# Eight expert weight slots in place of six, with the loop's buffers in the mixer's feature buffer

## The chip, the cores and the metric

The kernel runs on one core of a Trainium2 chip. The metric is device time in microseconds of one launch; three runs of the kernel before gave 1341.48, 1341.05 and 1335.37 us, median 1341.05. One execution more was taken with the hardware profiler; every row below comes from it.

## The reference

Two layers of a hybrid trunk over 384 tokens (128 context, 256 latent) with 1024 features. Each layer has a token mixer (layer 0: a gated linear recurrence beside a long convolution; layer 1: two kinds of attention) and then a mixture of experts, which is what the change touches. All values are fp32.

```python
def hier_moe(h, w_grp, b_grp, w_rt, b_rt, w_gate, w_up, w_down):
    t = h.reshape(B * L, D)
    g_p, g_i = lax.top_k(jax.nn.softmax(t @ w_grp + b_grp), 1)      # 1 of 4 groups
    e_p, e_i = lax.top_k(softmax(logits of that group), TOP_K)      # 2 of its 4 experts
    ...
    a = jnp.einsum('td,edf->tef', t, w_gate)
    u = jnp.einsum('td,edf->tef', t, w_up)
    hid = jax.nn.silu(a) * u * gates[..., None]
    y = jnp.einsum('tef,efd->td', hid, w_down)
```

There are 16 experts a layer, each with three weight matrices of 1024 x 512 (gate, up) and 512 x 1024 (down).

## The kernel before

*Weight blocks.* All weights come in blocks of 128 x 4096 fp32 (2.097 MB), moved by SP's DMA queue. The mixers' projections and the adaLN weights (`in_proj`, 41 blocks) go through `ring`, three slots in turn (`load_blocks`, L531 to 543). An expert is three blocks (gate, up, down) of `in_moe`; a layer has 48 of them. Even experts use the three slots of `ring`, odd experts three more, `mo["ring"]`, which lie in `arena`, a scratch area of 22616 columns that the mixers use before (`carve`, L327). So six blocks can be held.

*Order of the loads* (`load_experts`, L545 to 580). The first block into `ring` waits for the last reader of one of its slots; then SP waits until the mixer's features are done (`features_mixed`) and an output has left the arena, issues three loads into the arena, and then two more into `ring` as its slots come free. After `table_ready` (the table of the first chunk of each expert) a loop over seven pairs of experts reloads a slot as soon as the expert that used it has passed the matmuls of that block (`gate_full`, `up_full`, `down_full`). SP is one queue in program order: a load behind a wait goes no earlier than that wait ends.

*Rows.* Tokens are routed to experts in chunks of 64 rows (`CAP`). POOL scatters all rows to `slots` in DRAM by an indirect DMA (L622), then loads chunk by chunk 64 x 1024 into `mo["rows"]` (L626, L634, L631), stores the results back (L639), and at the end gathers each token's two results (L648) into `picked`, on top of the arena slots. An expert has one or more chunks, by the data; a layer has 19 here.

*One chunk on the engines.* PE: 16 matmuls with the gate block and 16 with the up block (L1602; an fp32 matmul shows as two passes, so 64 rows), `turn` of the next chunk's rows by transposes (L1578), transposes of the hidden values (L1608), 8 matmuls with the down block (L1617, 16 passes). ScalarE copies the turned rows to `hS` (L785), applies SiLU (L794), copies the transposed hidden values (L800) and the output (L806). VectorE multiplies (L1291) and has nothing else in the loop. POOL may reload `rows` only when PE has turned both halves (`turned`, L630), and PE asks for the next chunk's rows ahead of the last step of the up block:

```python
if kind == 1 and k == KD - 1:
    pe.wait_ge(sems["rows_in"], g * 16 + 32)
```

PE and SP run a loop over pairs of experts around loops over chunks (L1588, L574); the loop bounds are read from the table (`first_chunk`, L516). After the loop PE transposes the token sums back (L1626) and VectorE adds them to `xT` (L1302). `cT` is the mixer's feature buffer, 3072 columns: the output projection (L1797) reads it last, and after the loop VectorE builds the token sums in it (L1296, L1297).

After layer 0's loop, SP loads layer 1's first three projection blocks (L540) as the last readers of `ring`, those of expert 14, are done.

Of the kernel before, what the change touches and what calls it, by code (L numbers as in the profile page):

```python
# [28 lines left out]
F32 = mybir.dt.float32  # L29
# [39 lines left out]
PROJ_SLOTS = 3  # L69

# [227 lines left out]
def trunk_kernel(nc, params_d, hypar_d, consts_d, hyconst_d, x_d, s0_d, ck_d, cv_d, dk_d, dv_d,  # L298
                 proj_d, moe_d, y_d, state_d, ock_d, ocv_d, odk_d, odv_d, slots_d):
    banks = plan_banks()  # L300
    with ExitStack() as ctx:
# [25 lines left out]
        def carve(shapes):  # L327

            out, at = {}, 0
            for name, shape in shapes:  # L330
# [4 lines left out]
                elif len(shape) == 3:  # L335
# [25 lines left out]
        mo = carve([("ring", (3, KD * HALF)), ("hS", (KD, CAP)), ("sg", (FHALF,)), ("hid", (FHALF,)),  # L361
                    ("hidT", (2, P)), ("rows", (D,)), ("out", (HALF,)), ("rk", (T,)),
# [5 lines left out]
                    ("posi", (TOP_K * NT,)), ("prime", (2,))])  # L368
        picked = mo["ring"].rearrange("p r n -> p (r n)")[:, 0 : TOP_K * NT * D].rearrange("p (s d) -> p s d", d=D)
# [6 lines left out]
        slot_loaded = [sem(f"slot_loaded{s}") for s in range(2 * PROJ_SLOTS)]  # L376
# [20 lines left out]
        loop_names = ("rows_in", "turned", "hS_ready", "gate_full", "up_full", "sg_ready", "hid_ready", "hidT_full",  # L397
# [86 lines left out]
        def slot_of(n):  # L484
# [3 lines left out]
            earlier = sum(1 for m in range(first) if m % PROJ_SLOTS == s) + (NE // 2 if layer else 0)  # L488
# [14 lines left out]
        def moe_block(side, kind):  # L503

            return (mo["ring"] if side else ring)[:, kind, :]

        def moe_loaded(side, kind):
            return slot_loaded[PROJ_SLOTS * side + kind]

        def moe_loads(layer, side, kind):  # L510

            if side:
                return layer * NE // 2
            return sum(slot_of(n)[0] == kind for n in range(sum(LAYER_BLOCKS[: layer + 1]))) + layer * NE // 2
# [9 lines left out]
        def _(sp):  # L524
# [1488 lines left out]
```

## Time and profile before

| what | value |
|---|---|
| three runs, median | 1341.05 us |
| the profiled execution, its own time | 1336.44 us |
| its span, first to last instruction | 1334.8 us |
| PE busy, matmuls | 1087.7 us |
| ScalarE, VectorE, POOL busy | 381.7, 319.8, 118.3 us |
| mean granted TensorE clock | 0.937 |
| DMA | 341.58 MB, 256 GB/s over the span |

Outside its span the profiled execution has 1.64 us. The page gives busy times for the whole span; its 40 slices of 33 us show two long stretches in which the DMA digit is 9, the two expert loops (L1602 starts at 469.57 us in layer 0 and at 1039.91 us in layer 1). Busy PE is not PE at its peak, and a share of the whole is a mean over stages. In the chain of waits each step names what the next one waited for; in the timelines a bracket behind a row gives the engine's idle time ahead of it and what ended it.

### The profile page before, as it was taken

To read this page: it belongs to the slowest core of one execution; us is meant where nothing else is said; L and a number is where in the kernel's file an instruction comes from. 1 tells how busy PE (TensorE), PEld (TensorE's weight loads), DVE (VectorE), ACT (ScalarE), POOL (GpSimd) and SP (SyncE) were. 2 spreads that over 40 slices of the span, in tenths; PEclk is the share of its full clock that TensorE was granted. 3 is DMA by queue.
4 is the path that set the end of the run, shared out by engine and by line. 5 is a ranking of instruction groups with operands and counts; after the bars stand their busy time and mean duration, and the time that the engine had idled before them with its cause. 6 is when DMAs were issued, how large, how long until landed. Compare 5 with 4: busy or idle time off the path is not lost.

```text
span 1334.8 us, 16405 instructions
## 1 busy us (share of the span) xinstructions
PE 1087.7 (81%) x6064; PEld 617.9 (46%) x6065; DVE 319.8 (24%) x869; ACT 381.7 (29%) x729; POOL 118.3 (9%) x201
## 2 busy tenths in 40 slices
PE   4899999889898299777997279899893897799991
PEld 1444545446454155444664044455551454365651
DVE  3332132433443200000000054555524000000003
ACT  4221101432323122122232046554632222222220
POOL 0000002000100211000110210000001010011112
PEclk9999999999999789888999689999996899999995
DMA  9644417641925749999999802221072699999984
GB/s 368 285 189 189 189 63 305 270 189 64 379 88 228 314 155 398 394 401 399 387 386 397 314 25 109 88 80 63 1 309 114 262 389 397 406 391 385 383 335 149
DMA packets 35287, 341.58 MB, mean 256 GB/s; under 512 B 4912, under 2 KB 6064, under 8 KB 17328
## 3 DMA queue, kind: packets, MB, share of 16 engines
q1 hardware_dynamic: 21744, 295.97, 56.0%
q0 software_dynamic: 13504, 45.10, 9.4%
q8 instruction: 24, 0.39, 0.1%
q14 instruction: 15, 0.12, 0.0%
HBM read 313.00 MB, written 28.05 MB: 256 GB/s over the span
## 4 chain that ended last, share of the span: by engine, by line
PE 57%; DMA 24%; DVE 7%; ACT 5%; issue 4%; POOL 2%; POOLq 0%; DVEq 0%; SPq 0%; ACTq 0%
PE bank L1602 12%; PE bank L1531 10%; DMA arena<-in_moe 10%; PE bank L1523 8%; DMA ring<-in_moe 6%; PE bank L1797 6%; PE bank L1617 5%; DMA arena<-slots 3%; DMA ring<-in_proj 2%; PE bank L1494 2%; PE bank L1508 2%; PE bank L1719 2%; DMA arena<-slots,arena 1%; POOL slots L622 1%; PE bank L1500 1%
## 5 line engine op out<-in xcount | busy, mean ns | idle before, releaser
L1531 PE MATMUL bank<-ring,hT 128*128 128x512 f32 x384 | 169.8, 597 | 5.5 <-ACT hT L732 4.3
L1602 PE MATMUL bank<-arena 128*64 128x256 f32 x1216 | 143.4, 392 | 27.2 <-DMA arena<-in_moe 25.4
L1602 PE MATMUL bank<-ring,arena 128*64 128x256 f32 x1216 | 146.1, 398 | 23.6 <-DMA ring<-in_moe 20.2
L1291 DVE TENSOR_TENSOR arena<-bank,arena 128x256 f32<-128x256 f32 x38 | 16.1, 425 | 545.2 <-PE bank L1602 545.2
L1602 PEld LDWEIGHTS bank<-arena 128*64 128x64 f32 x1216 | 100.5, 141 | 75.3 <-DMA arena<-in_moe 23.4
L1602 PEld LDWEIGHTS bank<-ring,arena 128*64 128x64 f32 x1216 | 101.3, 144 | 72.1 <-DMA ring<-in_moe 22.3
L1531 PEld LDWEIGHTS bank<-ring,hT 128*128 128x128 f32 x384 | 72.3, 192 | 91.7 <-issue 88.6
L1523 PE MATMUL bank<-hT,ring 128*128 128x384 f32 x320 | 108.0, 498 | 4.5 <-ACT hT L732 2.5
L785 ACT ACTIVATE arena<-bank 128x256 f32<-128x256 f32 x80 | 30.6, 383 | 234.3 <-PE bank L1578 234.0
L1797 PE MATMUL bank<-cT,ring 128*128 128x384 f32 x256 | 84.6, 487 | 0.0
L1523 PEld LDWEIGHTS bank<-hT,ring 128*128 128x128 f32 x320 | 61.9, 195 | 48.7 <-issue 6.5
L1617 PE MATMUL bank<-ring,arena 128*64 128x512 f32 x304 | 71.1, 609 | 3.0 <-DMA ring<-in_moe 0.9
L1617 PE MATMUL bank<-arena 128*64 128x512 f32 x304 | 69.4, 597 | 2.5 <-DMA arena<-in_moe 0.2
L1578 PE MATMUL bank<-con,arena 64*128 64x64 f32 x320 | 37.2, 239 | 41.5 <-DMA arena<-slots 41.5
L1797 PEld LDWEIGHTS bank<-cT,ring 128*128 128x128 f32 x256 | 47.9, 190 | 32.1 <-issue 0.9
L806 ACT ACTIVATE arena<-bank 128x512 f32<-128x512 f32 x38 | 22.7, 597 | 134.6 <-PE bank L1617 134.6
L1578 PEld LDWEIGHTS bank<-con,arena 64*128 64x128 f32 x320 | 26.5, 142 | 62.6 <-issue 62.6
L1626 PE MATMUL bank<-con,cT 128*128 128x128 f32 x48 | 9.7, 395 | 54.9 <-DVE cT L1297 54.9
L639 POOL DMA_DIRECT2D slots<-arena x76 | 40.8, 537 | 152.0 <-ACT arena L806 149.9
L794 ACT ACT_TABLE_LOAD x38 | 48.8, 1283 | 1.5 <-issue 0.8
L631 POOL DMA_DIRECT2D arena<-slots x38 | 20.0, 527 | 326.1 <-PE bank L1578 318.0
L1494 PE MATMUL bank<-ring,condT 128*32 128x512 f32 x384 | 46.3, 598 | 0.0
(268 smaller groups left out, 1134.9 us busy)
## 6 DMA issues: line engine op xcount, KB each, us to landing
ring<-in_moe SPq DMA_DIRECT2D x48, 2048.0 KB, 21.0
arena<-in_moe SPq DMA_DIRECT2D x48, 2048.0 KB, 22.4
ring<-in_proj SPq DMA_DIRECT2D x41, 2048.0 KB, 10.2
arena<-slots POOLq DMA_DIRECT2D x42, 256.0 KB, 8.8
slots<-arena POOLq DMA_DIRECT2D x76, 128.0 KB, 7.4
slots<-blank POOLq DMA_DIRECT2D x1, 7680.0 KB, 38.3
arena<-in_hyconst SPq DMA_DIRECT2D x1, 2432.0 KB, 14.7
xT<-in_x SPq DMA_DIRECT2D x1, 1536.0 KB, 11.5
```

What stands on the lines that cost most here:

```text
L639: pool.dma_start(slots_d[bass.ds(g * CAP, CAP), HALF * half : HALF * half + HALF], mo["out"][CAP * half : CAP * half + CAP, :]).then_inc(s ...
L785: nc.scalar.activation(mo["hS"][:, 4 * half : 4 * half + 4, :], psum[ROWS_BANK + half][:, 0 : 4 * CAP].rearrange("p (k n) -> p k n", k=4), ...
L794: nc.scalar.activation(mo["sg"], psum[GATE_BANK][:, 0:FHALF], ACT.Silu).then_inc(sems["sg_ready"], 1)
L1494: ins = mm(ps[rows, :], condT[:, k, :], w[:, k, :], start=k < 4, stop=k >= 4)
L1508: ins = mm(ps[:, 0:T], ones, hT[:, k, :], start=k == 0, stop=k == KD - 1)
L1523: ins = mm(ps[:, 0:T], w[:, k, P * m : P * m + P], src[:, k, :], start=k == 0, stop=k == KD - 1)
L1531: ins = mm(ps[:, :], src[:, k, P * i : P * i + P], w[:, k, :], start=k == 0, stop=k == KD - 1)
L1578: ins = nc.tensor.transpose(psum[ROWS_BANK + half][:, CAP * k : CAP * k + CAP], mo["rows"][0:CAP, P * (4 * half + k) : P * (4 * half + k) ...
L1602: ins = mm(psum[kind][CAP * half : CAP * half + CAP, 0:FHALF], mo["hS"][:, k, :], wk[:, k, FHALF * half : FHALF * half + FHALF], start=k = ...
L1617: ins = mm(psum[DOWN_BANK][CAP * half : CAP * half + CAP, :], mo["hidT"][:, b, CAP * fh : CAP * fh + CAP], wd[:, 2 * fh + b, HALF * half : ...
L1719: mm(ps[:, :], sc["el"][:, b, h, :], sc["vx"][:, h].rearrange("p j n -> p (j n)"), start=True, stop=True).then_inc(full_of("scan", u, f"U{ ...
L1797: ins = mm(ps[:, 0:T], w[:, k, P * j : P * j + P], cT[:, 4 * half + k, :], start=k == 0, stop=k == 3)
```

## The change

- `mo["ring"]` grows from three to five slots, so that with `ring` eight blocks are held (`MOE_SLOTS`). Block n of a layer's 48 goes to slot n modulo 8: five arena slots first, then the three of `ring` in the order in which its last projection blocks end (`ring_order`).
- `rows`, `hS`, `sg`, `hid` and `rk` move from the arena into `cT`. A new buffer `land` lies there too.
- Row loads go to `land`; VectorE copies `land` to `rows` once PE has turned the chunk before (`copy_rows`); POOL loads the next chunk when the copy is done, and PE waits for the copy.
- The loops over pairs are written out: PE has 16 loops over chunks, one for each expert, SP has 40 loads with fixed addresses.
- The first eight loads: SP waits for the mixer's features and the output's store first, issues the five arena loads, then the three into `ring`, each when its slot's last reader is done.
- Layer 1's first projection blocks now wait for expert 15, whose blocks lie in `ring`.
- `slots` has two chunks more, and they are cleared with the others; one row load more is issued a layer.

```diff
+ARENA_SLOTS = 5
+MOE_SLOTS = ARENA_SLOTS + PROJ_SLOTS
+MOE_BLOCKS = 3 * NE
...
-        mo = carve([("ring", (3, KD * HALF)), ("hS", (KD, CAP)), ("sg", (FHALF,)), ("hid", (FHALF,)),
-                    ("hidT", (2, P)), ("rows", (D,)), ("out", (HALF,)), ("rk", (T,)),
+        mo = carve([("ring", (ARENA_SLOTS, KD * HALF)), ("hidT", (2, P)), ("out", (HALF,)),
                     ("lg", (NT, 20)), ("l8", (NT, 8)), ("m8", (NT, 8)), ("i8", (NT, 8)), ("f8", (NT, 8)),
...
+        features = cT[:, :, :].rearrange("p k t -> p (k t)")
+        mo["rows"], mo["land"] = features[:, 0:D], features[:, D : 2 * D]
+        mo["hS"] = features[:, 2 * D : 2 * D + KD * CAP].rearrange("p (k n) -> p k n", k=KD)
+        mo["sg"] = features[:, 2 * D + KD * CAP : 2 * D + KD * CAP + FHALF]
+        mo["hid"] = features[:, 2 * D + KD * CAP + FHALF : 3 * D]
+        mo["rk"] = features[:, 2 * D + KD * CAP : 2 * D + KD * CAP + T]
         picked = mo["ring"].rearrange("p r n -> p (r n)")[:, 0 : TOP_K * NT * D].rearrange("p (s d) -> p s d", d=D)
...
+        def ring_order(layer):
+            end = sum(LAYER_BLOCKS[: layer + 1])
+            return [slot_of(n)[0] for n in range(end - PROJ_SLOTS, end)]
+        def moe_slot(layer, n):
+            v = n % MOE_SLOTS
+            return PROJ_SLOTS + v if v < ARENA_SLOTS else ring_order(layer)[v - ARENA_SLOTS]
+        def moe_block(layer, n):
+            v = n % MOE_SLOTS
+            return mo["ring"][:, v, :] if v < ARENA_SLOTS else ring[:, moe_slot(layer, n), :]
+        def moe_loads(layer, n):
+            s = moe_slot(layer, n)
+            proj = sum(slot_of(m)[0] == s for m in range(sum(LAYER_BLOCKS[: layer + 1])))
+            return proj + (layer * MOE_BLOCKS + n) // MOE_SLOTS + 1
...
-                def load(pair, kind, side):
-                    at_block = pair * 6 + (layer * NE * 3 + 3 * side + kind)
-                    sp.dma_start(moe_block(side, kind),
-                                 moe_d[bass.ds(at_block, 1)].rearrange("o p n -> p (o n)")).then_inc(moe_loaded(side, kind), 16)
-                def load_first(kind):
-                    full(sp, *last_group(last[kind]))
-                    load(0, kind, 0)
-                order = sorted(range(3), key=lambda kind: STREAM.index(last[kind]))
-                load_first(order[0])
+                sems = loops[layer]
+                def load(n):
+                    sp.dma_start(moe_block(layer, n),
+                                 moe_d[layer * MOE_BLOCKS + n]).then_inc(slot_loaded[moe_slot(layer, n)], 16)
                 features_mixed(sp, layer)
                 if layer == 0:
                     sp.wait_ge(state_out, 32)
                 else:
                     sp.wait_ge(cache_out, 64)
-                for kind in range(3):
-                    load(0, kind, 1)
-                for kind in sorted(order[1:]) if layer == 0 else order[1:]:
-                    load_first(kind)
-                sems = loops[layer]
+                for n in range(MOE_SLOTS):
+                    if n >= ARENA_SLOTS:
+                        full(sp, *last_group(last[moe_slot(layer, n)]))
+                    load(n)
                 sp.wait_ge(table_ready, layer + 1)
-                with sp.Fori(1, NPAIR) as i:
-                    for side in range(2):
-                        done = first_chunk(sp, i * 2 + (side - 1))
-                        for kind in range(3):
-                            sp.wait_ge(sems[("gate_full", "up_full", "down_full")[kind]], done)
-                            load(i, kind, side)
-                return first_chunk(sp, NE - 1)
+                ends = {}
+                for n in range(MOE_SLOTS, MOE_BLOCKS):
+                    expert, kind = (n - MOE_SLOTS) // 3, (n - MOE_SLOTS) % 3
+                    if kind == 0:
+                        ends[expert] = first_chunk(sp, expert + 1)
+                    sp.wait_ge(sems[("gate_full", "up_full", "down_full")[kind]], ends[expert])
+                    load(n)
+                return first_chunk(sp, NE)
...
+            def experts_done(slot):
+                kind = ring_order(0).index(slot)
...
-                pool.dma_start(mo["rows"][0:CAP, :], slots_d[0:CAP, :]).then_inc(sems["rows_in"], 16)
+                def load_rows(chunk):
+                    pool.dma_start(mo["land"][0:CAP, :], slots_d[bass.ds(chunk * CAP, CAP), :]).then_inc(sems["rows_in"], 16)
+                load_rows(0)
                 chunks = first_chunk(pool, NE)
-                def load_rows(chunk):
-                    pool.wait_ge(sems["turned"], chunk * 2)
-                    pool.dma_start(mo["rows"][0:CAP, :], slots_d[bass.ds(chunk * CAP, CAP), :]).then_inc(sems["rows_in"], 16)
-                pool.wait_ge(sems["turned"], 2)
-                pool.dma_start(mo["rows"][0:CAP, :], slots_d[CAP : 2 * CAP, :]).then_inc(sems["rows_in"], 16)
+                for chunk in (1, 2):
+                    pool.wait_ge(sems["rows_copied"], chunk)
+                    load_rows(chunk)
                 with pool.Fori(0, chunks) as g:
-                    load_rows(g + 2)
+                    pool.wait_ge(sems["rows_copied"], g + 3)
+                    load_rows(g + 3)
...
+                def copy_rows(chunk):
+                    dve.wait_ge(sems["rows_in"], chunk * 16 + 16)
+                    V.tensor_copy(mo["rows"][0:CAP, :], mo["land"][0:CAP, :]).then_inc(sems["rows_copied"], 1)
+                copy_rows(0)
+                dve.wait_ge(sems["turned"], 2)
+                copy_rows(1)
                 with dve.Fori(0, first_chunk(dve, NE)) as g:
                     dve.wait_ge(sems["hidT_full"], g + 1)
                     dve.wait_ge(sems["sg_ready"], g + 1)
                     dve.wait_ge(sems["up_full"], g + 1)
                     V.tensor_tensor(mo["hid"], psum[UP_BANK][:, 0:FHALF], mo["sg"], ALU.mult).then_inc(sems["hid_ready"], 1)
+                    dve.wait_ge(sems["turned"], g * 2 + 4)
+                    copy_rows(g + 2)
...
-                def weights_loaded(pair, kind, side):
-                    pe.wait_ge(moe_loaded(side, kind), pair * 16 + 16 * (moe_loads(layer, side, kind) + 1))
-                pe.wait_ge(sems["rows_in"], 16)
...
+                pe.wait_ge(sems["rows_copied"], 1)
...
+                for e in range(NE):
+                    w = [moe_block(layer, 3 * e + kind) for kind in range(3)]
+                    with pe.Fori(first_chunk(pe, e), first_chunk(pe, e + 1)) as g:
+                        for kind, done in ((0, "gate_full"), (1, "up_full")):
+                            weights_loaded(3 * e + kind)
...
+                                    pe.wait_ge(sems["rows_copied"], g + 2)
```

How instructions stand now, at three places. SP ahead of layer 0's loop (`bank_free` and `state_out` stand for the mixer's features and the output's store, each `bank_full` for the last matmuls of a block that held the slot); before:

```order
L540 DMA ring<-in_proj 128x4096 [waits bank_full5]
L551 DMA ring<-in_moe 128x4096 [waits bank_full5]
L551 DMA arena<-in_moe 128x4096 [waits bank_free0,state_out,bank_free4,bank_free3]
L551 DMA arena<-in_moe 128x4096 x2
L551 DMA ring<-in_moe 128x4096 [waits bank_full1]
L551 DMA ring<-in_moe 128x4096 [waits bank_full7]
L574 UNCONDITIONAL_BRANCH [waits table_ready]
```

and now:

```order
L556 DMA ring<-in_proj 128x4096 [waits bank_full5]
L567 DMA arena<-in_moe 128x4096 [waits bank_free0,state_out,bank_free4,bank_free3]
L567 DMA arena<-in_moe 128x4096 x4
L567 DMA ring<-in_moe 128x4096 [waits bank_full5]
L567 DMA ring<-in_moe 128x4096 [waits bank_full7]
L567 DMA ring<-in_moe 128x4096 [waits bank_full1]
L534 TENSOR_LOAD arena [waits table_ready]
```

The arena's loads have moved ahead of the first `ring` slot's wait, and are five. VectorE in layer 1's loop (`up_full`, `sg_ready`, `hidT_full` are the matmuls, the SiLU and the bank of the hidden values); before:

```order
L1286 UNCONDITIONAL_BRANCH
L1286 ISA
L1291 TENSOR_TENSOR arena<-bank,arena 128x256 [waits up_full1,sg_ready1,hidT_full1]
L1286 REGISTER_ALU
L1286 COMPARE_AND_BRANCH
```

and now, from the copies ahead of the loop on:

```order
L1300 COPY cT<-cT 64x1024 [waits rows_in1,dve_link]
L1300 COPY cT<-cT 64x1024 [waits rows_in1,turned1]
L534 TENSOR_LOAD arena
L534 ISA x2
L1305 UNCONDITIONAL_BRANCH
L1305 ISA
L1310 TENSOR_TENSOR cT<-bank,cT 128x256 [waits up_full1,sg_ready1,hidT_full1]
L1311 ISA
L1299 ISA [waits turned1]
L1300 COPY cT<-cT 64x1024 [waits rows_in1]
L1305 REGISTER_ALU
L1305 COMPARE_AND_BRANCH
```

A copy with two waits has come behind each multiplication, and the next multiplication stands behind it. POOL in layer 0 from the first row load on; before:

```order
L626 DMA arena<-slots 64x1024 [waits rows_placed]
L518 TENSOR_LOAD arena
L518 ISA x2
L634 DMA arena<-slots 64x1024 [waits turned0]
L635 UNCONDITIONAL_BRANCH
L635 ISA
L631 ISA [waits turned0]
L631 DMA arena<-slots 64x1024
L639 ISA [waits out_ready0]
L639 DMA slots<-arena 64x512
```

and now:

```order
L637 DMA cT<-slots 64x1024 [waits rows_placed]
L534 TENSOR_LOAD arena
L534 ISA x2
L637 DMA cT<-slots 64x1024 [waits rows_copied0] x2
L644 UNCONDITIONAL_BRANCH
L644 ISA
L637 ISA [waits rows_copied0]
L637 DMA cT<-slots 64x1024
L647 REGISTER_ALU
L649 ISA [waits out_ready0]
L649 DMA slots<-arena 64x512
```

Each row load waits for VectorE's copy in place of PE's turn, and one load more goes ahead of the loop.

## Rows read from the trace of the kernel before

**Rows 1.** The page, parts 1 and 4: PE's busy time; chain by engine.

```profile
PE 1087.7 (81%) x6064; PEld 617.9 (46%) x6065; DVE 319.8 (24%) x869; ACT 381.7 (29%) x729; POOL 118.3 (9%) x201
...
PE 57%; DMA 24%; DVE 7%; ACT 5%; issue 4%; POOL 2%; POOLq 0%; DVEq 0%; SPq 0%; ACTq 0%
```

**Rows 2.** Windows: stretch, length, busy of PE, PEld, DVE, ACT, POOL; clock, DMA, GB/s.

```profile
500.00:740.00 240.00, 207.14 (x1494) 122.27 (x1492) 7.22 (x17) 56.15 (x100) 26.24 (x49) 0.96 1.01 395
1060.00:1290.00 230.00, 203.16 (x1506) 123.72 (x1504) 7.22 (x17) 57.64 (x101) 27.10 (x51) 0.99 1.01 394
```

**Rows 3.** The chain that ended last, layer 0's loop: start us, us, what.

```profile
668.33 3.65 PE bank L1617 x16
...
680.47 3.65 PE bank L1617 x16
...
703.36 28.93 DMA arena<-in_moe
...
737.60 3.67 PE bank L1617 x16
...
743.21 8.73 DMA slots<-arena
```

**Rows 4.** The same chain, the end of layer 1's loop.

```profile
1298.05 3.68 PE bank L1617 x16
1303.67 2.47 DMA slots<-arena
```

**Rows 5.** Waits of PE in layer 0's loop: us in total, times, longest us.

```profile
PE bank L1602 <- DMA arena<-in_moe: 14.3, 5, 3.3
PE bank L1602 <- DMA ring<-in_moe: 11.7, 4, 3.0
PE bank L1608 <- DVE arena L1291: 4.4, 19, 0.2
```

**Rows 6.** Waits of PE in layer 1's loop.

```profile
PE bank L1602 <- DMA arena<-in_moe: 11.0, 5, 3.2
PE bank L1602 <- DMA ring<-in_moe: 8.5, 4, 2.9
...
PE bank L1602 <- DMA arena<-slots: 2.6, 3, 1.2
```

**Rows 7.** Timeline of SP's queue at five places: start us, us from first to last.

```profile
418.11 0.33 SPq L551 DMA_DIRECT2D ring<-in_moe  x1
418.62 1.36 SPq L551 DMA_DIRECT2D arena<-in_moe  x3
442.64 0.80 SPq L551 DMA_DIRECT2D ring<-in_moe  x2
...
488.03 0.34 SPq L551 DMA_DIRECT2D ring<-in_moe  x1
...
711.88 12.37 SPq L540 DMA_DIRECT2D ring<-in_proj  x3
...
1046.09 3.77 SPq L551 DMA_DIRECT2D ring<-in_moe  x2
```

**Rows 8.** Timeline of POOL, scatter and first row load, layer 0 and layer 1.

```profile
448.90 1.04 POOL L622 DMA_INDIRECT slots<-hT,arena  x1 [30.46 <-DVE arena L1263]
...
463.70 0.58 POOL L626 DMA_DIRECT2D arena<-slots  x1 [6.87 <-DMA slots<-hT,arena]
...
1023.30 1.00 POOL L622 DMA_INDIRECT slots<-hT,arena  x1 [27.74 <-DVE arena L1263]
...
1034.46 0.55 POOL L626 DMA_DIRECT2D arena<-slots  x1 [3.26 <-DMA slots<-hT,arena]
```

**Rows 9.** Timeline of VectorE behind layer 0's gather.

```profile
765.48 0.75 DVE L1296 TENSOR_SCALAR cT<-arena 128x1024 f32<-128x1024 f32 x1 [28.89 <-DMA arena<-slots,arena]
```

**Rows 10.** The page, part 3, DMA queues: packets, MB, share of 16 engines.

```profile
q8 instruction: 24, 0.39, 0.1%
```

**Rows 11.** Timeline of PE, the first matmuls of layer 0's expert 1.

```profile
496.33 6.67 PE L1602 MATMUL bank<-arena 128*64 128x256 f32 x60
```

More of the change, by code:

```diff
@@ L375, in trunk_kernel @@
         s0_in, caches_in = sem("s0_in"), sem("caches_in")
-        slot_loaded = [sem(f"slot_loaded{s}") for s in range(2 * PROJ_SLOTS)]
+        slot_loaded = [sem(f"slot_loaded{s}") for s in range(MOE_SLOTS)]
         bank_full = [sem(f"bank_full{b}") for b in range(BANKS)]
@@ L487, in slot_of @@
             s = (n - first) % PROJ_SLOTS
-            earlier = sum(1 for m in range(first) if m % PROJ_SLOTS == s) + (NE // 2 if layer else 0)
+            earlier = sum(1 for m in range(first) if m % PROJ_SLOTS == s) + (MOE_BLOCKS // MOE_SLOTS if layer else 0)
             return s, earlier + (n - first) // PROJ_SLOTS + 1
@@ L501, in last_group @@
             return (*name, KD - 1)
[L503 to L514, printed above, removed]
+        def ring_order(layer):
[11 more added lines that the diff above has]
+            return proj + (layer * MOE_BLOCKS + n) // MOE_SLOTS + 1
         def first_chunk(eng, expert):
@@ L1580, in turn, with weights_loaded @@
                     ins.then_inc(sems["turned"], 1)
[L1582 to L1585 removed]
+                def weights_loaded(n):
+                    pe.wait_ge(slot_loaded[moe_slot(layer, n)], 16 * moe_loads(layer, n))
+                pe.wait_ge(sems["rows_copied"], 1)
                 for half in range(2):
                     turn(half)
[L1588 to L1619 removed]
@@ new lines, in experts @@
+                for e in range(NE):
[3 more added lines that the diff above has]
+                            weights_loaded(3 * e + kind)
+                            wk = w[kind].rearrange("p (k n) -> p k n", k=KD)
+                            for k in range(KD):
+                                if kind == 0 and k % 4 == 0:
+                                    pe.wait_ge(sems["hS_ready"], g * 2 + (k // 4 + 1))
+                                if kind == 1 and k == KD - 1:
+                                    pe.wait_ge(sems["rows_copied"], g + 2)
+                                for half in range(2):
+                                    ins = mm(psum[kind][CAP * half : CAP * half + CAP, 0:FHALF], mo["hS"][:, k, :],
+                                             wk[:, k, FHALF * half : FHALF * half + FHALF], start=k == 0, stop=k == KD - 1)
+                            ins.then_inc(sems[done], 1)
+                        turn(0)
+                        pe.wait_ge(sems["hid_ready"], g + 1)
+                        for b in range(2):
+                            ins = nc.tensor.transpose(psum[HIDT_BANK][:, P * b : P * b + P], mo["hid"][:, P * b : P * b + P], ident)
+                        ins.then_inc(sems["hidT_full"], 1)
+                        turn(1)
+                        weights_loaded(3 * e + 2)
+                        pe.wait_ge(sems["hidT_ready"], g + 1)
+                        pe.wait_ge(sems["out_ready"], g + 1)
+                        wd = w[2].rearrange("p (f n) -> p f n", f=NF)
+                        for n, (b, fh) in enumerate(((0, 0), (0, 1), (1, 0), (1, 1))):
+                            for half in range(2):
+                                ins = mm(psum[DOWN_BANK][CAP * half : CAP * half + CAP, :], mo["hidT"][:, b, CAP * fh : CAP * fh + CAP],
+                                         wd[:, 2 * fh + b, HALF * half : HALF * half + HALF], start=n == 0, stop=n == NF - 1)
+                        ins.then_inc(sems["down_full"], 1)
@@ L2005 @@
     args += [nc.dram_tensor("out_" + n, s, F32, kind="ExternalOutput").ap() for n, s in outs.items()]
-    slots = nc.dram_tensor("slots", (CAP * (MAX_CHUNKS + 2), D), F32, kind="Internal").ap()
+    slots = nc.dram_tensor("slots", (CAP * (MAX_CHUNKS + 4), D), F32, kind="Internal").ap()
     trunk_kernel(nc, *args, slots)
```

37 lines of the change are left out of this document (3 added, 34 removed).

## Prediction

> **What bounds the kernel now.** The page comes first: TensorE is busy 81% of the span, and the chain that ended last is 57% PE and 24% DMA [rows 1]. Such a share is a mean over stages, so the two expert loops, where nearly all the edits lie, are read by themselves. The reader should look at the last two columns of the windows: over 240 us of layer 0's loop and 230 us of layer 1's, the DMA engines are busy all the time (1.01) and move 395 and 394 GB/s, while PE has 207 of 240 and 203 of 230 us [rows 2]. So the transfers fill the loop, and PE doesn't. The waits of PE say the same from the other side: it stands 14.3 + 11.7 = 26.0 us for weight blocks in layer 0's loop and 11.0 + 8.5 = 19.5 us in layer 1's [rows 5, 6]. The chain shows it where it counts, at the end: in layer 0 a weight transfer of 28.93 us stands ahead of the last chunk, whose last matmuls start at 737.60; in layer 1 they start at 1298.05 [rows 3, 4].
>
> A balance of bytes tests this reading. The first refill of a slot is issued at 488.03 in layer 0 and at 1046.09 in layer 1 [rows 7]; all loads issued earlier had landed while PE was still on its first chunks. After it 48 - 6 = 42 blocks of 128 x 4096 fp32 (2.097 MB) must come, 2.097 / 0.395 = 5.31 us each, 223.0 us. The 19 chunks of a layer (PE waits 19 times for the hidden values [rows 5]) each read and write 64 rows of 4 KB, 0.524 MB or 1.33 us, 25.2 us. Together 248.2 us. Measured from first refill to last down projection: 737.60 - 488.03 = 249.6 us and 1298.05 - 1046.09 = 252.0 us. The loop lasts as long as its bytes.
>
> **The change, part by part.**
>
> *Eight slots.* Eight blocks are now loaded ahead of the loop, so 40 and not 42 come after the first refill: 2 x 5.31 = 10.6 us less in each layer, **-21.2 us**. Two things must hold. First, the two extra blocks must fit where the DMA is idle. In layer 0 the five arena loads no longer stand behind a ring slot's last reader, the output projection that let the first loads go at 418.11 and 418.62 [rows 7]; at the earliest they can follow the last projection block. The last two ring slots are still freed at 442.64 at the latest, and what comes after them is two blocks, about 11 us, against the first refill at 488.03. In layer 1 the eighth block has from the output projection to 1046. Second, PE must not become the bound. A chunk takes 680.47 - 668.33 = 12.14 us where nothing is late [rows 3], and of the 26.0 and 19.5 us of waits 15.4 and 8.9 are left after 10.6 are gone. That is cover enough.
>
> *Less crowding ahead of layer 0's loop.* The scatter of rows starts at 448.90 and the first row load goes at 463.70, 14.8 us later; in layer 1 it takes 1034.46 - 1023.30 = 11.2 us [rows 8]. The difference of 3.6 us is the weight blocks: those issued at 442.64 still run during layer 0's scatter. Now the arena's five have gone earlier and only about half a block is left. Ends: 0 and -3.6; I take **-3.0**, near the second, since layer 1's row is the same scatter with a free DMA.
>
> *Rows landed, then copied.* The first chunk's rows now pass VectorE before PE turns them: one copy of 64 x 1024 fp32 a layer on the path. The nearest row is VectorE's 128 x 1024 fp32 operation with one input, 0.75 us [rows 9]; with a hop, 0.85. Ends: half of it, as for half the partitions, and double. Two layers: **+1.7** (0.8 to 3.4). The other copies lie in VectorE's loop behind the turn. They have most of a chunk before PE asks for the rows, and VectorE has 7.22 us of work in 240 [rows 2]. POOL's load of the next rows waits for the copy, about 0.85 us later than for the turn, and the store behind it on POOL waits longer for ScalarE's output anyway: nothing. A row load may now take a whole chunk. It ended PE's waits for 2.6 us in layer 1 [rows 6]; that goes, but the next wait, for weights, comes last: nothing, at most -3.
>
> *Layer 1's first projection blocks.* Before, SP issued three of them from 711.88 on [rows 7], behind the last expert's blocks. Now the last expert sits in the ring, and all three wait for its down projection, since the first in SP's order does. They then cross the last store, which took 8.73 us in layer 0 beside such blocks but 2.47 in layer 1 without [rows 3, 4], and the gather behind it. The store already paid; the gather now pays too, for at most the part of 3 x 5.31 = 15.9 us that outlasts the store, shared half: 0 to +4, I take **+1.0**, since most of it passes during the store. The projection itself comes after gather, token sums and norm, with its weights there.
>
> *Experts written out, the blank rows, buffers moved.* PE loses the backward branch of the pair loop and SP its address arithmetic, neither on a path that ends anything. Clearing 0.5 MB more of rows is 1.3 us of transfer, hidden in the scans. The loop buffers sit in the mixer's features, which are dead between the output projection and the token sums. All 0, with +1 as the end for the clearing. New code must be fetched, though: see the second rival.
>
> Sum: -21.2 - 3.0 + 1.7 + 1.0 = **-21.5 us**. Against the profiled execution's 1336.44 that is 1314.9. The runs shown have their median 4.6 us above it (1341.05, from 1335.37 to 1341.48); not knowing on which side the next median falls I add half, 2.3 us: **1317 us**, and 2.3 is added to the rivals as well.
>
> One rule bears on the size of the main term. The loops move 395 and 394 GB/s [rows 2], and 5.31 us a block comes from that. The Trainium skill ("DMA: Bandwidth & Descriptors", Specifications) states a limit of about 358 GB/s from memory for one core; by it the two blocks would be an estimated 11.7 us a layer and the sum -23.7. The rows are above that limit, so they decide.
>
> **Rivals.**
>
> *PE partly takes over.* The waits left, 15.4 and 8.9 us, hold only if chunks stay at 12.14 us. If fresh code costs PE 1 us an expert, 16 us a layer, the layers gain 26.0 - 16 = 10 and 19.5 - 16 = 3.5 us; with the small terms -13.8, 1325 us. For it: layer 1's margin is thin. Against: nothing yet shows such a stall.
>
> *Instruction fetch ends up slower.* Before, two expert bodies were run eight times; now PE runs sixteen in a row, each for the first time, while the DMA is full. If PE stood at each for a small transfer's trip, for which the nearest row is the 2.47 us of the last store [rows 4], a layer would pay 16 x 2.47 = 39.5 us. It turns slower where that passes the waits it can hide in: above 26.0/16 = 1.6 us an expert in layer 0 and 19.5/16 = 1.2 in layer 1. At 2.47 it is +13.5 and +20.0, with the small terms +33, 1372 us. For it: 24 instruction fetches in the whole run now, and many more then [rows 10]. Against: the second body was fresh once, at 496.33 with the DMA full, and its matmuls show no idle time ahead of them [rows 11]. The Trainium skill ("Runtime: NRT & Kernel Launch", Instruction fetch mechanics) says that prefetch is sequential and that a taken branch out of the window stalls; by that rule written-out code is the safe form, and the row agrees.
>
> *More than the bytes.* Row waits, and PE's slower matmuls behind a weight wait, also go from the end of the chain: about 5 us more, 1312 us.
>
> *The slots don't help.* If the DMA fell idle in the loop because a slot is freed late, or the two blocks were not loaded ahead, the loop would start with the same debt: 1338 us. Against: the issue order gives the arena five loads without a wait among them.
>
> **How the numbers follow.** Forecast 0.65, more than the bytes 0.08, PE partly takes over 0.14, no help 0.07, slower 0.06. A measurement of this kernel can tell about 0.5%, 6.7 us, from no change. The forecast, the larger gain and nearly all of the partial one lie beyond: faster 0.86; same 0.08; slower 0.06. The range takes in the forecast with its ends (all low terms: -21.2 - 3.6 + 0.8 - 3 = -27; all high: -21.2 + 3.4 + 4 + 1 = -12.8), on either level of the runs shown, and the partial case: 1308 to 1328.
>
> **What would show it.** Right: eight weight loads issued before the first refill and 40 after, DMA share 1.0 at about 395 GB/s until the end, first refill to last down projection about 239 us, PE's waits for weights down by about 10 us a layer, the first row load 11 to 12 us after the scatter begins. Wrong: idle gaps of PE at each expert's first matmul that no transfer ends, a DMA share below 1 in the loop, row loads or copies ending PE's waits, or a tail of layer 0 longer by over 4 us.

## The result and the profile after

The kernel after takes 1327.78 us (median of seven runs, 1323.98 to 1330.71), the kernel before 1340.80 (seven runs); ratio 0.9916, 95% interval 0.9897 to 0.9935. It is faster, by 0.84% or 11.3 us, where 21.5 were forecast. (The two medians lie 13.0 us apart; from here on the text goes by the ratio.) The profiled execution of after has a span of 1325.9 us.

The page of after, busy time and the DMA queue that fetches instructions [rows 1, 10]:

```profile
PE 1085.3 (82%) x6064; PEld 618.7 (47%) x6064; DVE 348.5 (26%) x911; ACT 381.8 (29%) x729; POOL 119.2 (9%) x203
...
PE 59%; DMA 24%; DVE 7%; ACT 5%; issue 3%; POOL 2%; POOLq 0%; DVEq 0%; ACTq 0%
...
q8 instruction: 46, 0.75, 0.2%
```

SP's queue around layer 0's loop and at the start of layer 1's, as [rows 7]:

```profile
399.58 2.44 SPq L567 DMA_DIRECT2D arena<-in_moe  x5
419.72 25.70 SPq L567 DMA_DIRECT2D ring<-in_moe  x3
487.69 12.46 SPq L567 DMA_DIRECT2D arena<-in_moe  x4
...
734.02 1.28 SPq L556 DMA_DIRECT2D ring<-in_proj  x3
...
1042.53 15.92 SPq L567 DMA_DIRECT2D arena<-in_moe  x5
```

Eight loads go ahead of the first refill, as said; five of them 19 us earlier than the first arena load of before. The chain that ended last, layer 0's end and layer 1's [rows 3, 4]:

```profile
687.34 36.36 DMA ring<-in_moe
723.74 5.03 PE bank L1622 x32
...
730.33 3.67 PE bank L1637 x16
...
735.95 7.75 DMA slots<-arena
...
751.04 8.60 DMA arena<-slots,arena
```

```profile
1282.44 5.38 PE bank L1622 x32
...
1289.39 3.67 PE bank L1637 x16
...
1295.01 2.45 DMA slots<-arena
```

So a weight transfer still stands ahead of layer 0's last chunk. From first refill to last down projection it is now 730.33 - 487.69 = 242.6 us and 1289.39 - 1042.53 = 246.9; before 249.6 and 252.0, forecast about 239. The loops got 6.9 and 5.1 us shorter, not 10.6 each. The windows of exactly these stretches, with the columns of [rows 2]:

```profile
487.69:730.33 242.64, 212.07 (x1572) 128.69 (x1569) 19.30 (x35) 59.27 (x106) 27.31 (x51) 0.98 0.99 384
1042.53:1289.39 246.86, 220.15 (x1663) 135.30 (x1659) 20.40 (x37) 62.69 (x112) 28.76 (x54) 0.99 0.99 379
```

The same stretches of before:

```profile
488.03:737.60 249.57, 216.36 (x1572) 128.70 (x1568) 7.65 (x18) 59.12 (x106) 27.30 (x51) 0.96 1.01 393
1046.09:1298.05 251.96, 222.63 (x1661) 135.91 (x1656) 8.07 (x19) 62.59 (x112) 28.75 (x54) 0.99 1.00 387
```

The last column is what to read: fewer bytes had to come, but they came at 384 and 379 GB/s in place of 393 and 387, with the DMA engines nearly as busy (0.99 against 1.01 and 1.00). Part of that lies at the loop's ends: from 500 to 720 us it is 392 against 394, from 1060 to 1280 us 387 against 393. PE's waits for weights tell the same; layer 0, then layer 1 [rows 5, 6]:

```profile
PE bank L1622 <- DMA arena<-in_moe: 16.3, 7, 3.6
PE bank L1622 <- DMA ring<-in_moe: 7.7, 3, 3.2
```

```profile
PE bank L1622 <- DMA arena<-in_moe: 9.6, 4, 3.5
PE bank L1622 <- DMA ring<-in_moe: 9.2, 4, 3.4
```

24.0 and 18.8 us, from 26.0 and 19.5: they have hardly fallen, where the prediction wanted about 10 less a layer. The waits for rows (0.5 and 2.6 us) are gone; most of what else the loops lost is PE's own time, 212.07 against 216.36 us and 220.15 against 222.63 for the same matmuls, in layer 0 at a higher granted clock (0.98 against 0.96). POOL's scatter and first row load [rows 8]:

```profile
452.31 1.04 POOL L632 DMA_INDIRECT slots<-hT,arena  x1 [32.27 <-DVE arena L1273]
...
463.48 0.56 POOL L637 DMA_DIRECT2D cT<-slots  x1 [3.24 <-DMA slots<-hT,arena]
```

11.2 us in place of 14.8. (What lies ahead of the scatter differs from one profiled execution to the next: over all kernels of this text it began between 446 and 454 us. So stretches are compared, not times from the start.)

### The profile page after: what moved, and what is told of

Read it like the earlier page. It is cut to its first block, busy times and chain, and to the rows that moved or that the text cites. A ratio compares the mean times of both kernels' runs of the same rounds, so it can differ in the third digit from the quotient of the medians.

```text
span 1325.9 us, 16236 instructions
## 1 busy us (share of the span) xinstructions
PE 1085.3 (82%) x6064; PEld 618.7 (47%) x6064; DVE 348.5 (26%) x911; ACT 381.8 (29%) x729; POOL 119.2 (9%) x203
## 4 chain that ended last, share of the span: by engine, by line
PE 59%; DMA 24%; DVE 7%; ACT 5%; issue 3%; POOL 2%; POOLq 0%; DVEq 0%; ACTq 0%
PE bank L1622 12%; DMA arena<-in_moe 11%; PE bank L1552 11%; PE bank L1544 8%; DMA ring<-in_moe 7%; PE bank L1637 6%; PE bank L1817 6%; DMA ring<-in_proj 2%; PE bank L1515 2%; PE bank L1529 2%; PE bank L1739 2%; DMA arena<-slots,arena 1%; POOL slots L632 1%; PE bank L1521 1%; PE bank L1674 1%
## 5 line engine op out<-in xcount | busy, mean ns | idle before, releaser
L1622 PE MATMUL bank<-arena,cT 128*64 128x256 f32 x1632 | 190.3, 390 | 27.4 <-DMA arena<-in_moe 25.9
L1622 PEld LDWEIGHTS bank<-arena,cT 128*64 128x64 f32 x1632 | 135.2, 141 | 87.8 <-issue 26.2
L1622 PE MATMUL bank<-ring,cT 128*64 128x256 f32 x800 | 93.7, 389 | 16.9 <-DMA ring<-in_moe 16.9
L795 ACT ACTIVATE cT<-bank 128x256 f32<-128x256 f32 x80 | 30.7, 384 | 218.1 <-PE bank L1599 217.8
L1622 PEld LDWEIGHTS bank<-ring,cT 128*64 128x64 f32 x800 | 65.8, 140 | 47.4 <-DMA ring<-in_moe 14.8
L1599 PE MATMUL bank<-con,cT 64*128 64x64 f32 x320 | 37.2, 239 | 39.6 <-DVE cT L1300 39.6
L1637 PE MATMUL bank<-ring,arena 128*64 128x512 f32 x240 | 54.8, 597 | 2.7 <-DMA ring<-in_moe 0.9
L637 POOL DMA_DIRECT2D cT<-slots x44 | 23.2, 527 | 356.7 <-DVE cT L1300 350.2
L1599 PEld LDWEIGHTS bank<-con,cT 64*128 64x128 f32 x320 | 26.5, 142 | 60.8 <-issue 60.8
L1300 DVE COPY cT<-cT 64x1024 f32<-64x1024 f32 x42 | 28.8, 685 | 75.9 <-PE bank L1599 38.1
## 6 DMA issues: line engine op xcount, KB each, us to landing
xT<-in_x SPq DMA_DIRECT2D x1, 1536.0 KB, 11.2
```

The lines of the kernel that those rows point to most:

```text
L795: nc.scalar.activation(mo["hS"][:, 4 * half : 4 * half + 4, :], psum[ROWS_BANK + half][:, 0 : 4 * CAP].rearrange("p (k n) -> p k n", k=4), ...
L1300: V.tensor_copy(mo["rows"][0:CAP, :], mo["land"][0:CAP, :]).then_inc(sems["rows_copied"], 1)
L1599: ins = nc.tensor.transpose(psum[ROWS_BANK + half][:, CAP * k : CAP * k + CAP], mo["rows"][0:CAP, P * (4 * half + k) : P * (4 * half + k) ...
L1622: ins = mm(psum[kind][CAP * half : CAP * half + CAP, 0:FHALF], mo["hS"][:, k, :], wk[:, k, FHALF * half : FHALF * half + FHALF], start=k = ...
L1637: ins = mm(psum[DOWN_BANK][CAP * half : CAP * half + CAP, :], mo["hidT"][:, b, CAP * fh : CAP * fh + CAP], wd[:, 2 * fh + b, HALF * half : ...
```

## The experiments

Each ratio is a kernel's time over that of the kernel before, run in the same round on the same chip. The rounds did not all run on one chip, so kernels of different rounds are compared by their ratios.

**First round: the change taken apart.** Theory: what the two extra slots give is about as forecast, and some other part of the change costs what is missing. Four kernels.

*six_slots*: the changed kernel with the old number of slots.

```diff
-ARENA_SLOTS = 5
+ARENA_SLOTS = 3
```

> The changed kernel with six slots in place of eight; all its other edits stay. From first refill to last down projection the kernel before took 249.6 us (layer 0) and 252.0 us (layer 1), the changed kernel 242.6 and 246.9, where 239 and 241 were forecast. Theory 'the other edits slow the transfers' (instruction fetch or row copies): the two loops come out 3 to 5 us longer than in the kernel before, 253 to 257 us, and the kernel is 0 to 1% slower than before. Rival 'eight blocks outstanding slow the transfers': the loops are as in the kernel before, 250 and 252 us, at 392 to 395 GB/s, and the time is within 0.3% of before.

1346.14 us, ratio 1.0044 (1.0022 to 1.0066): slower than before. Its loops are 252.2 and 258.0 us long, so with eight slots they are 9.5 and 11.1 us shorter: the main term of the sum (10.6 each) was right, and the rest of the change, forecast at -0.3 us, costs 0.44%.

*written_out_alone*: the kernel before, with PE's and SP's loops over pairs written out.

```diff
-                with sp.Fori(1, NPAIR) as i:
+                for i in range(1, NPAIR):
...
-                with pe.Fori(0, NPAIR) as i:
+                for i in range(NPAIR):
```

> The kernel before with its experts written out on TensorE and SP, six slots, nothing else. Theory 'instruction fetch takes from the transfers': about 22 fetches of 16 KB more, loops of 253 to 257 us in place of 249.6 and 252.0, GB/s in the loops down from 393 to 388, the kernel 6 to 9 us slower than before. Rival 'depth' and rival 'row copies': the same as before within 2 us, loops 250 and 252 us.

1344.74 us, 1.0037 (1.0016 to 1.0059). The edit that was priced at 0 costs about 5 us.

*landed_alone*: the kernel before, with `land`, VectorE's copies and the row loads that wait for them (the buffers stay in the arena).

```diff
+                    dve.wait_ge(sems["turned"], g * 2 + 4)
+                    copy_rows(g + 2)
...
-                    load_rows(g + 2)
+                    pool.wait_ge(sems["rows_copied"], g + 3)
+                    load_rows(g + 3)
```

> The kernel before with rows landed and then copied by VectorE, nothing else. If the copies or the earlier row loads disturb the weight transfers: loops of 253 to 257 us, the kernel 6 to 9 us slower. If they don't: the two first copies alone, 1 to 2 us slower than before, loops 250 and 252 us.

1340.35 us, 0.9998 (0.9972 to 1.0024): the copies cost nothing that can be told (the interval is -3.8 to +3.2 us, so the 1.7 us forecast fit as well).

*late_projection*: the changed kernel; SP holds layer 1's first projection loads until the gather has landed.

```diff
                 kind = ring_order(0).index(slot)
+                sp.wait_ge(picked_in, 16 * TOP_K * NT)
```

> The changed kernel, with layer 1's first three projection blocks loaded only after layer 0's gather has landed. In the changed kernel the last store took 7.75 us and the last gather 8.60 us behind its issue; in layer 1, with no such blocks, 2.45 and 6.52. Theory 'these blocks stand in the way of the tail': store 2.5 and gather 6.5, layer 0's tail 7 us shorter, the kernel 6 to 8 us faster than the changed one. Rival: the projection then waits for its weights (a block lands about 7 us after its issue) and takes the gain back; no more than 2 us faster.

1314.21 us, 0.9803 (0.9774 to 0.9832): ahead of both kernels, and of after by 1.1% in the ratio. SP and POOL behind layer 0's loop in it:

```profile
753.67 1.28 SPq L556 DMA_DIRECT2D ring<-in_proj  x3
```

```profile
740.11 0.19 POOL L654 TENSOR_TENSOR arena<-arena 128x1 f32<-128x1 f32 x1 [2.17 <-DMA slots<-arena]
```

and POOL at the same place in after:

```profile
743.95 0.19 POOL L653 TENSOR_TENSOR arena<-arena 128x1 f32<-128x1 f32 x1 [7.46 <-DMA slots<-arena]
```

In after the three blocks are issued at 734.02, ahead of the last store (735.95), so the store takes 7.75 us and the gather is crossed too. With them held, the wait for the store falls from 7.46 to 2.17 us and the stretch from the gather's first issue to the token sums from 15.0 (744.68 to 759.66) to 12.8. That is 7.4 us of the chain; layer 1's projection begins no later for it. The ratio shows more than these 7.4 us (1.1%, some 15). The profiled execution was the longest of its six, 1320.98 us, 6.5 below that of after. The granted clock goes along with the rest: the four shortest runs of late_projection (1311.63 to 1314.45) have a mean of 0.940 to 0.943, the two longest 0.933 and 0.934, after's seven 0.926 to 0.939. Whether the clock is the cause is open.

**Second round: which part of writing out.** Theories: instruction fetches, which come with PE's sixteen bodies; or SP's loads; or the buffers' place, since six_slots has a longer layer 1 loop than written_out_alone.

*pe_written_out* (only the PE line of the diff of written_out_alone):

> The kernel before with only PE's loop over pairs written out; SP keeps its loop. Question: writing out PE and SP together cost 0.37% (about 5 us) where the prediction had 0. Theory A (instruction fetch): the whole price comes with PE, since PE's sixteen bodies are the code that is new: 1343 to 1346 us, instruction fetches up from 24 to about 46, PE idle no longer at an expert's first matmul, the loops 2 to 3 us longer in total. Rival B (SP's written-out loads are the price, for instance because they are issued in another rhythm): 1340 to 1341 us, loops as before.

1345.49 us, 1.0038 (1.0015 to 1.0061), 46 fetches in place of 24.

*sp_written_out* (only the SP line):

> The kernel before with only SP's loop over pairs written out (fixed addresses); PE keeps its loop. Theory A (instruction fetch by PE's bodies): no change, 1339 to 1342 us, and at most a few more instruction fetches. Rival B (SP's loads are the price): 1343 to 1346 us.

1339.11 us, 1.0003 (0.9977 to 1.0029), 24 fetches. By these two the price is PE's.

*buffers_moved_alone*:

```diff
-        mo = carve([("ring", (3, KD * HALF)), ("hS", (KD, CAP)), ("sg", (FHALF,)), ("hid", (FHALF,)),
-                    ("hidT", (2, P)), ("rows", (D,)), ("out", (HALF,)), ("rk", (T,)),
+        mo = carve([("ring", (3, KD * HALF)), ("hidT", (2, P)), ("out", (HALF,)),
+        features = cT[:, :, :].rearrange("p k t -> p (k t)")
+        mo["rows"] = features[:, 0:D]
...
```

> The kernel before with rows, hS, sg, hid and rk in the mixer's feature buffer and nothing else changed. The change with six slots has 386 GB/s in layer 1's loop and a loop 6 us longer than before, the written-out kernel alone 392 and 0.8 us. Theory A (the buffers' place costs nothing, as predicted): 1339 to 1342 us, 393 to 395 GB/s in both windows. Rival C (the buffers' new place slows layer 1): 1344 to 1346 us, about 387 GB/s in layer 1's window.

1341.01 us, 1.0012 (0.9989 to 1.0035): nothing that can be told.

*late_projection_eight_bodies*: late_projection, with PE's experts as a loop of two over eight bodies (block n + 24 has the slot of block n, so eight is the smallest number with eight slots).

```diff
-                for e in range(NE):
+                with pe.Fori(0, 2) as i:
+                    for e in range(NE // 2):
```

> The changed kernel with layer 1's first three projection loads held until the gather has landed (1314.21 us by itself), and PE's sixteen experts as a loop of two over eight bodies, so that half of the code is new in each layer. Theory A (instruction fetch): fetches fall from 46 to about 34 and the loops get 1 to 3 us shorter in total, 1311 to 1313 us, a version ahead of both kernels. Rival D (the price isn't the code that is fetched): 1314 to 1315 us, or longer if the backward branch costs.

1316.81 us, 0.9812 (0.9772 to 0.9852), 34 fetches: no gain over late_projection. With 0.4% to either side the run could not have told the 1 to 3 us that were expected, so it decides nothing.

**Third round: PE's bodies in the changed kernel, and what a transfer on one engine costs.**

*six_slots_pair_loop*: six_slots with PE's loop over pairs put back, everything else as changed.

```diff
-                for e in range(NE):
+                with pe.Fori(0, NPAIR) as i:
+                    for e in range(2):
```

> The changed kernel with six slots (1346.14 us, ratio 1.0044) and PE's experts as the loop over eight pairs that the kernel before has; the moved buffers, landed rows, load order and SP's written-out loads stay. Theory A (PE's sixteen bodies are the price that the prediction set to 0): the 5 us go, and with the less crowded scatter that this kernel keeps it comes to 1338 to 1341 us, instruction fetches back to 24, each loop 250 to 252 us. Rival E (the price lies in the moved buffers, the copies and the load order taken together, since layer 1's loop took 258 us with six slots and 254 at most with PE written out alone): 1344 to 1346 us, layer 1's loop still 256 us or longer.

1336.93 us, 0.9981 (0.9966 to 0.9997): 9.2 us below six_slots, 8.4 by the ratios. Sixteen bodies are what the change loses by. The loops took 249.7 and 254.1 us in it, 252.2 and 258.0 in six_slots, though PE was busy for 6.4 us less in those; pe_written_out has 253.1 and 254.5, sp_written_out 250.5 and 251.5. (Layer 1's 254.1 is above the 250 to 252 expected.) PE's waits in layer 1 (1050 to 1285 us), in six_slots:

```profile
PE bank L1622 <- DMA arena<-in_moe: 12.9, 5, 3.8
PE bank L1622 <- DMA ring<-in_moe: 5.9, 3, 3.2
PE bank L1628 <- DVE cT L1310: 3.9, 17, 0.2
PE bank L1637 <- DMA arena<-in_moe: 2.0, 2, 1.9
PE bank L1637 <- DMA ring<-in_moe: 1.3, 2, 1.1
```

and in six_slots_pair_loop:

```profile
PE bank L1623 <- DMA arena<-in_moe: 9.8, 4, 3.1
PE bank L1623 <- DMA ring<-in_moe: 6.2, 2, 3.2
PE bank L1629 <- DVE cT L1310: 3.9, 17, 0.2
```

22.1 us of waits for weights against 16.0. PE does not stand at a new body; it stands for weights that come later. (The waits alone would be a weak sign: they also grow when PE runs at a higher clock, and sp_written_out, which costs nothing, has 20.9 us of them in this stretch at a clock of 1.00.) The windows, 500 to 720 and 1060 to 1280 us, six_slots:

```profile
500.00:720.00 220.00, 184.63 (x1350) 108.43 (x1348) 16.65 (x30) 51.20 (x90) 24.10 (x45) 0.97 1.01 393
1060.00:1280.00 220.00, 192.70 (x1418) 115.59 (x1416) 17.75 (x32) 53.11 (x95) 24.94 (x48) 0.97 1.01 386
```

and six_slots_pair_loop:

```profile
500.00:720.00 220.00, 192.90 (x1384) 113.94 (x1382) 16.64 (x30) 53.13 (x92) 25.74 (x48) 0.95 1.01 397
1060.00:1280.00 220.00, 198.06 (x1441) 121.57 (x1442) 17.90 (x33) 54.99 (x97) 25.58 (x48) 0.96 1.01 391
```

397 and 391 GB/s against 393 and 386, at the same DMA share. These two kernels ran on different chips; on one chip, pe_written_out has 391 and 393 in the two windows and sp_written_out 392 and 393, so the lower rate is not shown to be the code's. Nor do the loops hold all of the price: of the 9.9 us between the two spans 6.4 lie in the loops and 3.5 ahead of the scatter, where no expert body has run yet; pe_written_out and sp_written_out differ by 5.6 us in the loops and 7.1 ahead of the scatter. Whether the part ahead is a difference between executions or belongs to the code is open. In the trace eleven more fetches lie in each loop, packets of 16.4 KB that take 1.0 to 1.3 us apiece.

*small_loads_one_row* and *small_loads_spread* measure what such a transfer does, without new code on PE: sp_written_out with one small load more behind each refill, 16.4 KB in one row, or in 16 rows. What they bring is read by nobody; nothing of the computation is left out. Behind each loop SP and VectorE wait once for the small loads.

```diff
                             load(i, kind, side)
+                            n = (i - 1) * 6 + side * 3 + kind
+                            sp.dma_start(mo["spare"][n : n + 1, :], moe_d[layer * NE * 3 + n, 0:1, :]).then_inc(small_in, 16)
```

> The kernel before with SP's loop written out (no change in time by itself), and one small load more behind each of the 42 refills of a layer: one row of 4096 fp32, 16.4 KB, the size of an instruction fetch, into an unused part of the arena that nothing reads. Rival F (a small transfer costs its bytes): 42 x 16.4 KB = 0.69 MB, 1.75 us a loop at 394 GB/s, 3.5 us in all, 1343 us. Theory A (a transfer that sits on one DMA engine holds up the weight blocks, which are spread over all sixteen; 11 more fetches cost about 2 us a loop, 0.2 us each): 42 x 0.2 = 8 us a loop, 16 us in all, 1356 us.

> The same 42 small loads a layer and the same bytes, but each as 16 rows of 1 KB, so that they can be spread over the DMA engines. Rival F (bytes): 1.75 us a loop, 1343 us, as with one row. Theory A (one engine is held up): clearly less than with one row, 1341 to 1346 us against about 1356 us. If both are alike and well above 1343 us, it is the number of transfers in SP's queue that costs, and neither theory is shown.

One row: 1404.51 us, 1.0493 (1.0471 to 1.0515). Spread: 1356.22, 1.0118 (1.0086 to 1.0150). The loops last 282.6 and 284.9 us with one row, 261.5 and 263.3 spread, 250.5 and 251.5 without. Layer 0's loop, one row, then spread, then sp_written_out:

```profile
490.00:765.00 275.00, 220.41 (x1528) 126.49 (x1524) 7.21 (x17) 58.22 (x103) 27.32 (x51) 0.93 0.92 355
```

```profile
490.00:745.00 255.00, 216.02 (x1526) 122.48 (x1524) 7.21 (x17) 58.09 (x102) 27.33 (x51) 0.95 1.01 381
```

```profile
490.00:735.00 245.00, 208.05 (x1530) 123.78 (x1528) 7.21 (x17) 58.08 (x102) 27.30 (x51) 0.98 1.01 392
```

By bytes both would cost 1.75 us a loop. Spread they cost about 11 (0.27 us each), in one row about 33 (0.78 us each), and the DMA share falls to 0.92, as it would if some engines stood while one is behind. Both came out dearer than expected (1356 and 1341 to 1346 us); what the spread load's 0.27 us is made of is open. So transfers of one packet cost far more than their bytes where the loop lives on the DMA, which is how fetches could cost 9 us. It does not show that they do.

**Fourth round: the price by the number of bodies.** *six_slots_four_bodies* and *six_slots_eight_bodies* are six_slots_pair_loop with `pe.Fori(0, NE // 4)` over four bodies and `pe.Fori(0, NE // 8)` over eight.

> The changed kernel with six slots and PE's experts as a loop of four over four bodies; with sixteen bodies it took 1346.14 us (ratio 1.0044, 46 instruction fetches), with two bodies in a loop of eight 1336.93 us (0.9981, 24 fetches). Theory A (each instruction fetch beside the weights costs): the time follows the fetches; four bodies give about 28, so 0.4 us each times 4 more: ratio 0.999, 1338 to 1339 us. Rival G (the price is not the fetch but something that comes with any body that is not among the two, such as where the code lies): already near the sixteen bodies, 1.003 to 1.005, 1344 to 1346 us.

> The same with a loop of two over eight bodies, about 34 fetches. Theory A: 10 more fetches than with two bodies at 0.4 us each, ratio about 1.001, 1341 us, between the two ends. Rival H (the price is only there where every body is met once, and a loop over eight costs nothing): 0.998, 1337 us. Rival G: 1.004, 1346 us, as with sixteen.

| bodies | fetches | both loops, us | median us | ratio to before (95%) |
|---|---|---|---|---|
| 2 | 24 | 503.7 | 1336.93 | 0.9981 (0.9966 to 0.9997) |
| 4 | 27 | 502.9 | 1339.70 | 1.0008 (0.9984 to 1.0032) |
| 8 | 34 | 508.5 | 1344.18 | 1.0036 (1.0014 to 1.0059) |
| 16 | 46 | 510.1 | 1346.14 | 1.0044 (1.0022 to 1.0066) |

The medians rise with each step; clear of noise are eight and sixteen bodies above two, while neighbouring steps overlap. So the price goes with how much code PE runs. Rival H (only code that is met once costs) falls with eight bodies; rival G (any new body costs all) is unlikely, with four bodies at 1.0008 and its 1.003 at the edge of their interval. Proportion to the fetches is not borne out: ten of the 22 extra ones go with 7.3 of the 9.2 us, and a straight line from two to sixteen bodies would give 1.0010 for eight, just below that interval. But the line's two ends have noise of their own, so it is not ruled out either. What else grows with the bodies is not in the trace.

## Why the prediction was wrong

By ratios to before, the change comes apart into three steps: everything but slots and bodies (six_slots_pair_loop) -0.19%, 2.5 us; sixteen bodies 1.0044 - 0.9981 = +0.63%, 8.4 us (0.36 to 0.90% with both intervals); eight slots 0.9916 - 1.0044 = -1.28%, 17.2 us (13.3 to 21.1). Together -11.3 us, as measured. So of the 10.2 us that are missing from the forecast 8.4 are the bodies' and 4.0 the slots' (within their interval), and the small terms gave 2.2 more than forecast. The kernel before shows a smaller price for the same bodies (pe_written_out, +0.38%, 0.15 to 0.61); the two intervals overlap.

- *The bound* was read rightly: two blocks less to load made the loops 9.5 and 11.1 us shorter, and small loads added beside them made them longer.
- *Eight slots, -21.2*: the loops got 9.5 and 11.1 us shorter against six_slots, 20.6 together; by the ratios -17.2, with the forecast at the edge of its interval. Held; with it falls the rival by which the slots don't help.
- *Less crowding, -3.0*: 14.8 to 11.2 us, -3.6. Held.
- *Landed rows, +1.7*: not to be told from 0, nor from 1.7; a copy takes 0.69 us on VectorE, and one a layer lies on the path.
- *Layer 1's first projection blocks, +1.0*: the stretch from last down projection to token sums grew from 27.9 us (737.60 to 765.48) to 29.3 (730.33 to 759.66), +1.4; as far as layer 1's first refill the growth is 3.7 (308.5 to 312.2). Held, as a difference. What it missed is that before already paid: with the loads held, 7.4 us of store and gather go in all.
- *Experts written out, the blank rows, buffers moved, "All 0"*: **the step that failed.** Buffers and SP's part are 0, PE's sixteen bodies are +8.4 us. The text counted a branch less and looked for new code only where PE would stand at it. That stall is not there: PE's waits in after's loops name weights, VectorE and, once a loop, ScalarE; no stop at a new body is among them. PE at the second expert in after, with no idle time ahead of its gate matmuls [rows 11]:

```profile
494.43 1.92 PE L1637 MATMUL bank<-arena 128*64 128x512 f32 x8
496.14 7.11 PE L1622 MATMUL bank<-arena,cT 128*64 128x256 f32 x64
```

  The second rival (1372 us) falls with it. A third possibility, that more code slows the transfers beside it, was not on the list, though the text itself held both halves: a loop bound by the DMA, and fetches that are DMA transfers. It is what the runs leave as the likeliest.
- *PE partly takes over, 1325 us* came near in time and by the wrong road: PE's waits were still 24.0 and 18.8 us, so it took over nothing.
- *The base*: the profiled execution lay 4.4 us below the median of before (1340.80), of which half was added: 2.1 us more.

The Trainium skill ("Runtime: NRT & Kernel Launch", Instruction fetch mechanics) calls the cost of going from one block of code to the next mostly hidden. For PE's own time the trace agrees, since no stall is seen. For the whole kernel written-out code costs 8.4 us, though no run shows that crossing blocks is what costs it. Shown is that the price comes with PE's code, and that PE does not stand at it. That it appears as later weights rests on the longer loops of two pairs of traces, which hold some half to two thirds of it. That the fetches themselves carry it is argued from the small loads, and stays open by the uneven steps from two to sixteen bodies.

## What to carry to other kernels

Where a loop lasts as long as its bytes, a block loaded before it begins is worth its whole transfer time, and so is moving a transfer off a stretch where a short one is waited for: holding three loads until the gather had landed took the ratio from 0.9916 to 0.9803. In such a loop do not count on anything that uses the DMA being free, the fetching of code perhaps among it: price a written-out loop by a run with the loop alone written out. A small load should be spread over all DMA engines, or not be there.

## What was not expected of the hardware

- A load of one row of 16.4 KB beside the weights cost 0.78 us, the same bytes in 16 rows 0.27, by their share of the bytes 0.04. The page's queues show 168 packets more for the 84 one-row loads and 2688 for the spread ones: 2 and 32 each. A 16.4 KB packet takes 0.67 us in this loop on average, so 42 of them one after the other on one engine would make 28 of the 33 us, an estimate. The Trainium skill ("DMA: Bandwidth & Descriptors", on why a DMA raises its semaphore by 16) says that a transfer from SP that uses few engines takes the lowest-numbered ones, so that loads on one engine would all meet on the same. No row names the engine; the DMA share of 0.92 agrees.
- Eight bodies in a loop of two were fetched once a layer (six_slots_eight_bodies): six fetches of 16.4 KB lie in each expert loop, all of them in its first half.
- The last chunk's up matmuls, behind the loop's last wait for weights, ran at a granted clock of 0.73 (layer 0) and 0.68 (layer 1) in after and at 1.00 in before's layer 0, 5.03 and 5.38 us against 3.70 for 32 of them. PE had stood 3.23 and 3.35 us just ahead of them in after, 3.00 in before. The windows, two of after and one of before, with the columns of [rows 2]:

```profile
723.70:728.80 5.10, 5.06 (x34) 2.91 (x35) 0.00 (x0) 0.00 (x0) 0.00 (x0) 0.73 0.58 242
1282.40:1287.80 5.40, 5.36 (x33) 3.08 (x34) 0.00 (x0) 0.00 (x0) 0.00 (x0) 0.68 0.53 225
...
732.00:737.00 5.00, 4.42 (x38) 2.73 (x38) 0.42 (x1) 0.39 (x1) 0.00 (x0) 1.00 1.00 427
```

The first two are means between the clock's two levels, 2.4 and 1.2 GHz. It is not what sixteen bodies cost: six_slots_pair_loop has it too, 5.10 and 5.15 us for the same 32 matmuls. What decides it is open; it is worth some 1.5 us a loop.
